# Sixteen bytes further: where the two halves of the normalised input begin in on-chip memory

## The reference

```python
def swiglu(h, w_gu, w_out):
    gu = h @ w_gu
    return (jax.nn.silu(gu[..., :FFN_DIM]) * gu[..., FFN_DIM:]) @ w_out

for i in range(DEPTH):                       # DEPTH = 4
    h = rms_norm(x, attn_norm[i])
    ...                                      # h @ w_qkv, attention, @ w_o
    x = x + mix
    x = x + swiglu(rms_norm(x, ffn_norm[i]), f_w_gu[i], f_w_out[i])
```

## Time and profile before

| | |
|---|---|
| median of 3 runs | 2425.86 us (2424.44 to 2426.05) |
| the profiled execution | 2419.68 us, of which its span 2417.5 us |
| mean granted TensorE clock | 0.962 of full speed |
| PE busy | 2281.9 us (94%), 18326 matmuls |
| PE weight loads busy | 2198.2 us (91%) |
| DVE busy | 1552.3 us (64%) |
| ACT busy | 1144.0 us (47%) |
| POOL busy | 345.8 us (14%) |
| DMA | 150 GB/s on average |

### The profile page before, as it was taken

The page is one execution under the profiler, slowest core; times in us unless marked ns, Lnnn a source line. Parts: engine busy times, 40 slices in busy tenths (PEclk is TensorE's granted clock), DMA queues, the critical chain, the costliest instruction groups (busy, mean ns, idle before and its releaser), DMA issues.

```text
span 2417.5 us, 45763 instructions
## 1 busy us (share of the span) xinstructions
PE 2281.9 (94%) x18326; PEld 2198.2 (91%) x18326; DVE 1552.3 (64%) x2040; ACT 1144.0 (47%) x1477; POOL 345.8 (14%) x448
## 2 busy tenths in 40 slices
PE   8999997999999999999999998988899998889998
PEld 7899997799999999999989997886899988868998
DVE  6865547466467776564776545767677456966764
ACT  5653344544355555443564434435365353445552
POOL 0011100021000000210301210840012029000110
PEclk9999998999999999999999999988999999989999
DMA  6356533166544444565435653532456543524651
GB/s 211 124 146 186 191 121 133 43 172 190 192 157 151 140 154 143 158 190 192 152 123 157 187 187 105 167 109 100 122 156 188 189 130 105 175 69 127 187 191 70
DMA packets 431038, 362.12 MB, mean 150 GB/s; under 512 B 20524, under 2 KB 404144, under 8 KB 430904
## 3 DMA queue, kind: packets, MB, share of 16 engines
q1 hardware_dynamic: 429128, 358.79, 48.2%
q0 software_dynamic: 1264, 0.71, 0.1%
q10 hardware_dynamic: 512, 0.72, 0.1%
HBM read 359.12 MB, written 1.05 MB: 149 GB/s over the span
## 4 chain that ended last, share of the span: by engine, by line
PE 79%; DVE 9%; POOL 6%; ACT 3%; issue 1%; DMA 0%; SPq 0%; ACTq 0%; POOLq 0%; DVEq 0%
PE bank L470 69%; POOL hT L1315 4%; DVE weights_lo L1835 3%; POOL Z L1317 2%; PE bank L573 2%; PE bank L817 1%; PE bank L501 1%; PE bank L831 1%; ACT weights_hi L1353 1%; PE bank L708 1%; PE bank L947 1%; PE bank L979 1%; PE bank L730 1%; PE bank L960 1%; PE bank L754 1%
## 5 line engine op out<-in xcount | busy, mean ns | idle before, releaser
L470 PE MATMUL bank<-h_hi,weights_hi 128*128 128x256 f32 (+1 forms) x3728 | 1067.6, 286 | 54.4 <-DVE weights_lo L1835 17.2
L1835 DVE TENSOR_TENSOR weights_lo<-weights,weights_hi 128x2048 fp32r<-128x2048 f32 x343 | 787.8, 2297 | 497.9 <-ACT weights_hi L1353 495.3
L470 PE MATMUL bank<-h_lo,weights_hi 128*128 128x256 f32 (+1 forms) x3728 | 1056.6, 283 | 0.0
L470 PE MATMUL bank<-h_hi,weights_lo 128*128 128x256 f32 (+1 forms) x3728 | 1055.7, 283 | 0.0
L1353 ACT CAST weights_hi<-weights 128x2048 fp32r<-128x2048 f32 x343 | 655.3, 1911 | 535.9 <-PE bank L470 527.5
L470 PEld LDWEIGHTS bank<-h_hi,weights_hi 128*128 128x128 f32 (+1 forms) x3728 | 716.2, 192 | 65.5 <-issue 49.0
L470 PEld LDWEIGHTS bank<-h_lo,weights_hi 128*128 128x128 f32 (+1 forms) x3728 | 716.6, 192 | 1.5 <-issue 1.4
L470 PEld LDWEIGHTS bank<-h_hi,weights_lo 128*128 128x128 f32 (+1 forms) x3728 | 716.0, 192 | 0.0
L470 PE MATMUL bank<-hid_hi,weights_hi 128*128 (+1 forms) x1056 | 294.7, 279 | 0.0
L470 PE MATMUL bank<-hid_lo,weights_hi 128*128 (+1 forms) x1056 | 294.7, 279 | 0.0
L470 PE MATMUL bank<-hid_hi,weights_lo 128*128 (+1 forms) x1056 | 294.7, 279 | 0.0
(11 more groups left out here) (316 smaller groups left out, 2622.6 us busy)
## 6 DMA issues: line engine op xcount, KB each, us to landing
weights<-in_f_w_gu SPq DMA_DIRECT2D x176, 512.0 KB, 4.9
weights<-in_f_w_out SPq DMA_DIRECT2D x88, 512.0 KB, 4.2
weights<-in_w_up SPq DMA_DIRECT2D x88, 512.0 KB, 4.9
weights<-in_w_in SPq DMA_DIRECT2D x82, 512.0 KB, 4.4
weights<-in_c_w_qkv SPq DMA_DIRECT2D x72, 512.0 KB, 4.4
weights<-in_a_w_qkv SPq DMA_DIRECT2D x48, 512.0 KB, 4.5
weights<-in_w_down SPq DMA_DIRECT2D x44, 512.0 KB, 4.2
weights<-in_a_w_o SPq DMA_DIRECT2D x16, 512.0 KB, 4.1
```

The lines of the kernel that those rows point to most:

```text
L470: mm = nc.tensor.matmul(out, x, y, start=(first and n == 0), stop=(last and n == 2), skip_group_check=True)
L1835: v_.tensor_tensor(w_lo[slot][:], raw[slot][:], w_hi[slot][:].bitcast(F32), ALU.subtract).then_inc(lo_ready, 1)
```

## The change

Each of the two buffers is made 8 numbers (32 bytes) longer, and what the program calls `h_hi` and `h_lo` is the part of it that begins 4 numbers (16 bytes) behind its start. No instruction is added, removed or moved on any engine, and each has its old form; the addresses in them are what differs. The remainders are in the table above: the two buffers leave the 32-byte grid and stay on the 16-byte grid, and the others keep their remainder by 64.

```diff
@@ -149,8 +149,8 @@
         xT = sb("xT", [P, KT, T])
         hT = sb("hT", [P, KT, T])
         lams = sb("lams", [P, 4])
-        h_hi = sb("h_hi", [P, KT, T], F32R)
-        h_lo = sb("h_lo", [P, KT, T], F32R)
+        h_hi = sb("h_hi", [P, KT * T + 8], F32R)[:, 4:KT * T + 4].rearrange("p (m n) -> p m n", n=T)
+        h_lo = sb("h_lo", [P, KT * T + 8], F32R)[:, 4:KT * T + 4].rearrange("p (m n) -> p m n", n=T)
         sq = sb("sq", [P, KT, T])
         pres = sb("pres", [P, 6 * T])
         rots = sb("rots", [P, 4 * T])
```

## The result

| | before | after |
|---|---|---|
| median of 13 executions each, same chip | 2423.87 us (2422.14 to 2430.81) | 2432.0 us (2427.73 to 2442.58) |
| ratio, 95% interval | | 1.0035, 1.0023 to 1.0046 |
| the profiled execution, its span | 2419.68, 2417.5 us | 2431.27, 2429.1 us |
| mean granted TensorE clock | 0.962 | 0.961 |

The change makes the kernel slower by 8.1 us, 0.35%, outside the 0.2% that I called no change. My time of 2425.9 us was that of no change; the range of 2421 to 2467 holds the result, the range of 2422 to 2430 that I gave for no change does not. Ratios and intervals are worked out over the executions of both kernels and not from the two medians, from which they can differ by 0.1%; one execution of the kernel before beside runs 8 to 11, of 6074 us, is left out of them.

The account below looks back on a forecast made before the run. The prediction took PE's back-to-back matmuls to bound the kernel; moving reads, stationary reads, writes and other buffers each cost 0, so 2425.9 us against the median of 2425.86, with a range of 2421 to 2467 us.

Parts of the forecast that it names:

- one more unit per read: Rival: PE fetches 32-byte units, so each moving read of h needs 33, not 32; 40.8 us, 2466.7 us; chance 0.25, whole or part.
- The other buffers: Term for the buffers other than h: they move by 64 bytes, keep their remainder by 64, weights stay; cost 0.
- A start in the middle of a 64-byte piece costs a matmul nothing that these rows resolve: Step on moving reads: matmuls with starts at remainders 0 and 32 were read as equally fast; cost 0.
- the excess over the clock: Matmul distance of 116.7 ns, 10 ns over 256 columns at 2.4 GHz; claimed not to depend on the start.
- the shift by 64 of all later buffers: Rival: a 128-byte grid slows up to all 18,326 matmuls by one column each; 8.4 us, 2434.3 us; chance 0.04.
- the split: Rival: 16-byte lines are fetched in pairs only on the grid, so h's stream halves; 1,088 us, 3514 us; chance 0.03.
- reads in units of 64 bytes: Step on moving reads: 64-byte units, where a mid-piece start would touch 17 and not 16, were called ruled out.
- the new start suits PE better: Rival: shifting h by 16 parts weight load and stream in memory; 59 us less, 2366.6 us; faster by either way 0.06.
- the moving reads of h: Term for the 11,184 matmuls with h moving: starts off the 32-byte grid cost 0 ns.
- the stationary reads: Term for the 1,080 weight loads of h: may grow some 5 ns before it is seen; cost 0.
- the writes: Term for ACT writing h_hi and DVE writing h_lo off the grid: cost 0, bound 1.3 us.
- the reading of the bound: Claim that PE, busy 94% of the span, bounds the kernel, so added matmul distance adds to the time at once.

Follow-up runs that it names:

- runs 8 to 11: Run 8, run 9, run 10 and a scan of the kernel before, h and hid per part at other starts, halves equal by 512 bytes: 2433.79 us.
- run 2: Kernel before with 64 bytes added behind h_lo: h untouched, everything behind it moved by 64 bytes; 2431.08 us against 2422.48, ratio 1.004.
- run 10: Kernel before with 64 bytes ahead of the rounded weights, so weights, h, hid and o all move 64 bytes together; 2423.17 us against 2424.69, ratio 0.9999.
- run 1: Changed kernel with another 64 bytes behind h_lo, so everything behind h moves by 128 bytes in all; 2430.12 us against 2422.48, ratio 1.0039.
- run 8: Kernel before with h_hi and h_lo at 240 and hid_hi and hid_lo at 496 by 512 bytes; 2393.04 us against 2424.69, ratio 0.9859.
- Run 7: Kernel before with the rounded weights of the three slots at 128, 160 and 192 and every moving operand at 416; 2436.15 us.
- run 9: Changed kernel with four small buffers packed into one, so hid and o return to 160 while h stays at 176 and 208; 2425.33 us against 2424.69, ratio 1.0007.
- run 6: Scan of the kernel before in which each part takes h and hid at another start, h by a period of 256 bytes; 2424.86 us.

## Why the prediction was right and wrong

**The number held, the reasoning did not.** The change was to cost nothing and cost 8.1 us. That the stated range holds 2432.0 us is luck: its upper part was laid out for one more unit per read of h, and h paid nothing.

**The step that failed** is "The other buffers. They move by 64 bytes and keep their remainder by 64; the weights stay. Cost 0." That the weights stay was taken as harmless, and it is the cause: hid and o went 64 bytes further from the weights (run 2: ratio 1.004 by this alone; run 10: 0.9999 if the weights go along). The term was put at nothing. In the traces it was 3,162 x 3.31 ns = 10.5 us for hid and 2.6 us for o and the branches, of which 9.8 and 0.6 us reached the time; between the medians the whole change cost 8.1 us.

**Under it lies a wrong inference.** "A start in the middle of a 64-byte piece costs a matmul nothing that these rows resolve" compared starts across kinds of matmul: h on weights, weights on h, sq on ones. In the earlier trace rows both windows have the same distance of 32 bytes between moving and stationary start, so they could not differ. In the earlier trace rows roles and buffers are swapped together, and the 118.2 ns there, which I read as equal, are 1.5 ns more than 116.7. With 3,162 matmuls that is 4.7 us, the whole scale that I had set. And I wrote that if the excess over the clock were a matter of the start "it would have to differ between remainder 0 and 32, and it does not". It does depend on the start: it is 113.3 - 106.7 = 6.6 ns at the best place and 14.4 ns at the worst. The formula from the Trainium skill ("TensorE: Matmul & The Clock Gate", Back-to-back issue gap) that this was weighed against is given there for an isolated matmul, so that it doesn't cover a stream in which each matmul has its weight load.

**The rival "the shift by 64 of all later buffers"** had 0.04. It is what happened, and its sign in the profile (the hid window moves, the h window doesn't) was the right one to look for. Its size, 2434.3 us, is near the 2432.0 measured, but by chance: one column (0.46 ns) on all 18,326 matmuls is not 3.3 ns on some 4,100. Its mechanism, a grid of 128, fell in run 1. And what I held against it, that weights at multiples of 256 are no faster, spoke of the wrong thing, an absolute place.

**The rival "one more unit per read"** is refuted: the windows with h moving hold 859 and 860 matmuls, and run 8 has every h and hid read off the 32-byte grid and is the fastest. The same goes for the split. Nor was the reading right that the earlier trace rows rule out reads in units of 64 bytes: they can't settle it, since the start of the other operand differs in them too.

**The rival "the new start suits PE better"** was right in kind, not for these places: its reason, that weight load and stream meet in the same part of the memory, is the nearest of my sentences to what runs 7 and 10 show. At 240 the gain is 3.3 ns of the 5.3 that I gave as its bound. The bound itself was no lowest distance: transposes with 128 columns (moving ident, stationary sq) have a median of 109 ns in the same trace.

**Right were** the costs of 0 for the moving reads of h (run 9: 1.0007), for the stationary reads (117.7 ns before and 118.1 ns after with weights moving, 0.4 us in all) and for the writes, and the reading of the bound: PE's distance goes into the time at once. For the moving reads this was luck too. h went to 176/208, a pair that has the old pace; with both halves at 176 run 6 had 118.33 ns, which by an estimate from that value would have been 11,184 x 1.66 ns = 19 us.

## What to carry to other kernels

An edit that changes the length or place of one buffer moves every buffer behind it: list what has moved relative to what, and measure the edit once with the others held in place (run 9) and once without the edit itself (run 2) before its time is explained. Where a kernel is bound by back-to-back matmuls, read the distance between starts for each moving operand, since the median duration hid a loss of 3%. Then try starts of the moving buffers in steps of 16 bytes against those of the stationary ones, several in one kernel where it has repeated parts; take a place with one pace in all stretches, read from several executions, and look at the granted clock beside the time, since it can be lower in the faster kernel (0.954 against 0.962 here).

## What the runs showed of the hardware that was not expected

- float32r matmuls of 256 columns at the full granted clock (1.00, 2.4 GHz) are 113.3 to 121.1 ns apart, by the starts of moving and stationary operand relative to each other. Steps of 16 bytes change it by up to 7 ns either way. The 32-byte grid doesn't decide: 240 (113.4 ns) and 80 (119.2 ns) are off it, 320 (113.4 ns) and 224 (120.0 ns) on it.
- A placement can have two paces in one execution: 113.33 and 117.78 ns at 320, 113.5 and 117.78 ns at 192, 116.67 and 117.78 ns at 160. Run 2 even has one stretch of 192 matmuls at 120.1 ns with h at 160 (from 1727 us on). What switches it isn't known.
- The distance of one operand pair isn't all. The pair h_hi at 176 and h_lo at 208 ran at 116.8 ns, where thirds of 118.33 and 119.99 ns would give 118.9, although such thirds hold to 0.01 ns at 160/480 and 224/416. Which matmul follows which may count, or another pace of the same places; no run was made for it.
- The mechanism stays open. That weight loads and the moving stream meet in parts of the memory fits runs 7 and 10, but no run showed the meeting itself. The Trainium skill ("TensorE: Matmul & The Clock Gate", Step-by-step: what each phase is for) says that two independent read ports feed the moving operand and the weight load. Run 7, with 116.6, 119.8 and 118.3 ns for one moving buffer and three places of the weights, shows that the two operands' places set the pace together in this kernel, which two reads that have nothing to do with each other would not give.
